# Two projections in a 256-token trunk change how high and low parts meet on TensorE

## The chip, the cores and the metric

The kernel runs on one core of a Trainium2 chip. The metric is the device time of one execution in microseconds. The core has TensorE (PE, with its weight loads listed apart as PEld), VectorE (DVE), ScalarE (ACT), GpSimd (POOL) and SyncE (SP), which here issues all bulk transfers from device memory (HBM). TensorE reads operands from on-chip memory (SBUF) and writes into PSUM, which has 8 banks of 128 partitions x 512 float32 columns; VectorE and ScalarE read results out of PSUM.

## The reference

Two layers over 256 tokens of width 1024, all in float32. Each layer: a token mixer, cross-attention into 256 memory tokens, and a feed-forward block (dense in layer 0, a routed mixture of 8 experts in layer 1).

```python
for l in range(DEPTH):
    h = rmsnorm(x, g_mix[l])
    z = h @ w_in[l]                                   # 1024 -> 4096
    gates = sigmoid(z[..., o_g:])
    y_pool = pool_mixer(u_pool, w_pool_group[l], pool_scale[l]) @ w_pool_out[l]    # 512 -> 1024
    y_conv = (b_gate * short_conv(c_gate * u_conv, conv_w[l])) @ w_conv_out[l]     # 512 -> 1024
    merged = gates[..., :D_MODEL] * y_pool + gates[..., D_MODEL:] * y_conv
    x = x + merged @ w_mix_out[l]
    h = rmsnorm(x, g_xattn[l]);  mem_n = rmsnorm(mem, g_mem[l])
    x = x + cross_attention(h, mem_n, w_xq[l], w_xk[l], w_xv[l], w_xo[l])   # k = mem_n @ w_xk[l]
    h = rmsnorm(x, g_ffn[l])
    x = x + (swiglu(h, ...) if l % 2 == 0 else moe_ffn(h, ...))
return rmsnorm(x, g_final)
```

## The kernel before

**Split operands.** Every float32 operand of a large product is split into a high part (rounded to the fast matmul type) and a low part (the rest). A product is the sum of three passes: high x high, high x low, low x high. Weights arrive in *units* of 1 MB (128 x 2048 elements) in six raw buffers, loaded by SP in a fixed order. For each unit ScalarE copies the high part (`split_to`, tile whi) and VectorE subtracts it to get the low part (wlo); there are three whi/wlo pairs, so the high part of unit n waits until unit n-3 has been used by TensorE. TensorE waits for `lo_ready` of a unit before it starts it and raises `unit_used` at its end. The order on each engine is the order in which the code is written; the three engines walk through the same units with counters `p.u` (units), `p.c` (PSUM pairs) and `p.q` (transpose banks).

**PSUM.** Banks 0 to 5 form three pairs that are used in turn (`take_pair` waits for `pair_free`); banks 6 and 7 take transposes in turn (`take_bank` waits for `tp_free`).

**Two ways to multiply with transposed output.** `chunk_t` (lines 1364 to 1385) issues, for each of 16 (k, d) blocks of a unit, three matmuls with 256 columns each; high and low parts lie in separate tiles (mem_hi, mem_lo; b_hi, b_lo), and the whole result gathers in one place, so that one engine reads it once. It is used for K (`w_xk`, 4 units a layer) and for the two branch output projections (`w_pool_out`, `w_conv_out`, 4 units a layer, called B units below: B0 to B3). `chunk_wide` (lines 1387 to 1407) is used for `w_in`, `w_xq` and the dense gate and up: the activation's high and low parts lie side by side in a_parts, one matmul with 512 columns multiplies both by the weight's high part, and one with 256 columns multiplies the high part by the weight's low part. Its result lies in two halves, which ScalarE copies (`wide_side`) and VectorE adds (`wide_sum`).

**Around the B units.** Before them TensorE computes the last gates; after them come the `w_mix_out` units M0 to M3 (`chunk_n`). M0 needs `merged_ready` 1, M1 needs `merged_ready` 2. VectorE multiplies each B unit's result by its gates (L1088), for the last two adds the two branches (L1094), ScalarE copies the sum's high part into a_parts, and VectorE subtracts for the low part (L933), which raises `merged_ready`.

**The start.** The memory tokens are normalised, transposed four 128 x 512 groups at a time in banks 6 and 7 (two, then two more once VectorE has emptied the first), scaled and split into mem_hi and mem_lo (`evac_norm`), and the first K unit starts. `keep_clock` issues small matmuls whose results nobody reads.

**The experts.** After layer 1's attention SP streams 192 expert units of 1792 KB through a ring of 12 places; a place is refilled when TensorE has used it.

## Time and profile before

| | us |
|---|---|
| median of 3 runs (lowest, highest) | 1538.47 (1538.39, 1539.16) |
| time of the profiled execution | 1538.15 |
| its span (first to last instruction) | 1536.1 |
| PE, busy in the span | 1506.7 |
| PEld | 972.8 |
| DVE | 549.2 |
| ACT | 407.7 |

The span is 2.05 us shorter than the time of the same execution. The ends of matmuls are modelled and they overlap, so a busy TensorE may be waiting for a fraction of a microsecond; the distance between the starts of matmuls tells its pace better than its busy time.

### The profile page before, as it was taken

The numbers are of one execution on the slowest core, as the hardware profiler recorded it, in microseconds if no ns is written. First come the engines' busy times: TensorE is split into PE (matmuls) and PEld (weight loads), VectorE is DVE, ScalarE is ACT, GpSimd is POOL, SyncE is SP. The second block draws the span as 40 slices with busy tenths as digits, with TensorE's granted clock in tenths as the row PEclk, the third lists the DMA queues.
The fourth block names the chain that finished last, engine by engine and source line by source line (L and its number), as shares of the span: only waits on it lengthen the run. The fifth ranks groups of instructions, "written<-read, shape, count | busy, mean of one in ns | idle before, by whom it ended". The sixth has DMA issues, their size and how long they took to land. (4 is left out here: it accounts for less than half of the span.)

```text
span 1536.1 us, 31153 instructions
## 1 busy us (share of the span) xinstructions
PE 1506.7 (98%) x14375; PEld 972.8 (63%) x14375; DVE 549.2 (36%) x641; ACT 407.7 (27%) x512; POOL 32.2 (2%) x118
## 2 busy tenths in 40 slices
PE   8999999999999999999999999999999999999996
PEld 8889888988888889886354343443543434435433
DVE  5576666565566767552021110110211101101112
ACT  6445455544445454541000000000000000000001
POOL 1000000000000000103000000000000000000000
PEclk9999999999999999999999999999999999999998
DMA  9655653547566555667989999999999999999993
GB/s 339 206 176 187 230 167 110 164 166 228 163 210 195 164 193 190 241 275 309 403 354 405 425 425 427 423 426 425 425 425 425 425 425 425 425 425 425 425 425 163
DMA packets 124967, 478.68 MB, mean 312 GB/s; under 512 B 6212, under 2 KB 72868, under 8 KB 100260
## 3 DMA queue, kind: packets, MB, share of 16 engines
q1 hardware_dynamic: 124836, 476.68, 79.5%
q8 instruction: 113, 1.85, 0.5%
q14 instruction: 18, 0.15, 0.0%
HBM read 475.61 MB, written 1.05 MB: 310 GB/s over the span
## 5 line engine op out<-in xcount | busy, mean ns | idle before, releaser
L1721 PE MATMUL ps<-unit,h_slots 128*32 128x448 f32 x5376 | 511.2, 540 | 0.0
L1721 PEld LDWEIGHTS ps<-unit,h_slots 128*32 128x32 f32 x5376 | 173.0, 110 | 321.6 <-issue 318.4
L1403 PE MATMUL ps<-a_parts,whi 128*128 128x512 f32 x992 | 344.1, 396 | 0.0
L928 DVE TENSOR_TENSOR wlo<-raw,whi 128x2048 fp32r<-128x2048 f32 (+1 forms) x116 | 259.1, 2236 | 122.0 <-ACT whi L591 121.6
L1743 PE MATMUL ps<-unit,act_tok 128*32 128x256 f32 x4704 | 259.3, 380 | 11.4 <-DVE act_tok L1299 8.9
L1403 PE MATMUL ps<-a_parts,wlo 128*128 128x256 f32 x992 | 267.0, 280 | 0.0
L591 ACT ACTIVATE whi<-raw 128x2048 fp32r<-128x2048 f32 (+1 forms) x116 | 216.5, 1867 | 67.1 <-PE ps L1421 53.1
L1743 PEld LDWEIGHTS ps<-unit,act_tok 128*32 128x32 f32 x4704 | 151.3, 110 | 119.9 <-DVE act_tok L1299 12.3
L1403 PEld LDWEIGHTS ps<-a_parts,whi 128*128 128x128 f32 x992 | 182.9, 188 | 38.2
L1403 PEld LDWEIGHTS ps<-a_parts,wlo 128*128 128x128 f32 x992 | 187.1, 189 | 5.4
L1295 DVE TENSOR_TENSOR act_tok<-act_tok,ps 128x896 f32<-128x896 f32 x18 | 19.2, 1067 | 352.3 <-PE ps L1721 352.3
L591 ACT ACTIVATE y_slots<-ps 32x256 f32<-32x256 f32 x38 | 14.2, 373 | 329.1 <-PE ps L1743 328.7
L1256 DVE COPY y_slots<-ps 32x256 f32<-32x256 f32 x38 | 16.1, 423 | 193.7 <-PE ps L1743 193.2
L1421 PE MATMUL ps<-whi,a_parts 128*128 128x512 f32 x256 | 79.8, 393 | 1.1 <-DVE a_parts L933 1.1
L884 ACT ACTIVATE act_tok<-ps 128x896 f32<-128x896 f32 x18 | 16.5, 917 | 237.9 <-PE ps L1721 237.9
L1421 PEld LDWEIGHTS ps<-whi,a_parts 128*128 128x128 f32 x256 | 47.6, 188 | 11.3 <-issue 1.9
L1421 PE MATMUL ps<-wlo,a_parts 128*128 128x512 f32 x128 | 49.9, 390 | 0.0
L591 ACT ACTIVATE h_slots<-ps 128x384 f32<-128x384 f32 (+1 forms) x8 | 3.3, 465 | 143.8 <-PE ps L1697 142.4
L1269 DVE TENSOR_TENSOR x_res<-x_res,ps 128x512 f32<-128x512 f32 x28 | 18.0, 684 | 55.5 <-PE ps L1773 55.5
L1381 PE MATMUL ps<-mem_hi,whi 128*128 128x256 f32 x128 | 36.5, 285 | 0.0
L1381 PE MATMUL ps<-mem_hi,wlo 128*128 128x256 f32 x128 | 36.3, 283 | 0.0
L1381 PE MATMUL ps<-b_hi,wlo 128*128 128x256 f32 x128 | 36.3, 283 | 0.0
(256 smaller groups left out, 1241.6 us busy)
## 6 DMA issues: line engine op xcount, KB each, us to landing
unit<-in_w_e_gate SPq DMA_DIRECT2D x64, 1792.0 KB, 28.5
unit<-in_w_e_up SPq DMA_DIRECT2D x64, 1792.0 KB, 27.2
unit<-in_w_e_down SPq DMA_DIRECT2D x64, 1792.0 KB, 28.9
raw<-in_w_in SPq DMA_DIRECT2D x32, 1024.0 KB, 5.4
raw<-in_w_ff_gate SPq DMA_DIRECT2D x10, 1024.0 KB, 5.4
raw<-in_w_ff_up SPq DMA_DIRECT2D x10, 1024.0 KB, 5.3
raw<-in_w_xk SPq DMA_DIRECT2D x8, 1024.0 KB, 5.1
raw<-in_w_xv SPq DMA_DIRECT2D x8, 1024.0 KB, 5.1
```

The costliest lines, as they stand in the source:

```text
L591: return act.activation(dst, src, ACT.Copy, scale=scale)
L884: act.activation(dst, src, ACT.Silu).then_inc(s["silu_ready"], 1)
L928: dve.tensor_tensor(wlo[n % SPL][:, 0:size], raw[n % RAW][:, 0:size], whi[n % SPL][:, 0:size].bitcast(F32), ALU.subtract).then_inc(s["lo_r ...
L1256: ins = dve.tensor_copy(y_rows(g, q), y_piece(g, q))
L1269: dve.tensor_tensor(xs, xs, bank(SCATTER_BANKS[n]), ALU.add).then_inc(s["xadd_done"], 1)
L1295: dve.tensor_tensor(dst, dst, src, ALU.mult).then_inc(s["act_ready"], 1)
L1381: ins = pe.matmul(o[:, d, :], w[wi][:, k, d * P:(d + 1) * P], xs[xi][:, k0 + k, :], start=first and d % 2 == 0, stop=last, skip_group_chec ...
L1403: ins = pe.matmul(o if whole else o[:, 0:SEQ], w, x_, start=k == 0 and whole, stop=k == nk - 1 and whole, skip_group_check=True)
L1421: ins = pe.matmul(o[:, t, 0:nn], xs[xi][:, k0 + k, t * P:(t + 1) * P], w[wi][:, k, :], start=j == 0 and k == 0 and n == 0, stop=j == n_uni ...
L1721: ins = pe.matmul(ps[q * QP:(q + 1) * QP, 2 * h + f, 0:HC], he[:, k, c0 + h * QP:c0 + (h + 1) * QP], w[:, q * QC + f * HC:q * QC + (f + 1) ...
L1743: ins = pe.matmul(o[q * QP:(q + 1) * QP, h * 256:(h + 1) * 256], act_t[:, h, j * QP:(j + 1) * QP], unit_t[i - part + u][:, c0:c0 + 256], s ...
```

## The change

K and the B units move from `chunk_t` to the wide form. mem_hi and mem_lo become the two halves of mem_parts, b_hi and b_lo those of b_parts. K weights are loaded as tall units (all 8 k blocks x 256 columns, rows of 1 KB, in place of 4 k blocks x 512 columns, rows of 2 KB). `keys` reads K's results with a ScalarE copy and a VectorE sum for each unit. The B units use a new `chunk_wide_rows`: a unit fills two PSUM pairs, one after the other, and ScalarE and VectorE bring both into a scratch tile mix_tmp (which lies over b_gateT and win_sum1) before the gates are multiplied. At the start all four transpose groups go to four banks (6, 7, 4, 5) without a wait, `keep_clock` has 5 calls in place of 10 there (a call shows as two matmuls in the trace), and the first weight unit is split in two halves of 1024 columns.

`chunk_t` is gone.

```diff
-    add_square(a["w_xk"][0])
+    def add_keys(l):
+        for c in range(D // C):
+            add_tall(a["w_xk"][l], c * C, C)
+
+    add_keys(0)
...
         if l == 0:
-            add_square(a["w_xk"][1])
+            add_keys(1)
...
-    Ml = place("mem_lo", [P, KD, SEQ], F32R)
+    M = place("mem_parts", [P, KD, 2, SEQ], F32R)
+    Mh, Ml = M[:, :, 0, :], M[:, :, 1, :]
     kT = place("kT", [P, KD, SEQ], F32)
     moe_top = at["top"]
     gT = place("gatesT", [P, 2 * KD, SEQ], F32)
-    Bh = place("b_hi", [P, KD, SEQ], F32R)
-    Bl = place("b_lo", [P, KD, SEQ], F32R)
+    B = place("b_parts", [P, KD, 2, SEQ], F32R)
...
+    mix_tmp = [place(f"mix_tmp{i}", [P, NG, SEQ], F32, place_of[n]) for i, n in enumerate(("b_gateT", "win_sum1"))]
...
+        FIRST_BANKS = (6, 7, 4, 5)
+        HALF_UNIT = UNIT // 2
...
-                def evac_norm(dst, row, lo=0, hi=KD // 2):
+                def evac_norm(dst, row, lo=0, hi=KD // 2, banks=(6, 7, 6, 7)):
 
                     for kk in range(lo, hi):
                         act.wait_ge(s["tp_done"], p.q + 1)
-                        src = bank(6 + p.q % 2).rearrange("p (k t) -> p k t", k=2)
...
+                def pair_side(dst, scale=1.0):
+
                     src = pair(p.c).rearrange("p (d h t) -> p d h t", d=2, h=2)[:, :, 1, :]
                     copy(dst, src, scale).then_inc(s["wide_side"], 1)
                     p.c += 1
...
-                split_to(0)
-                evac_norm(Mh, G_MEM)
+                act.wait_ge(raw_loaded[0], 16)
+                copy(whi[0][:, 0:HALF_UNIT], raw[0][:, 0:HALF_UNIT]).then_inc(s["hi_half"], 1)
+                copy(whi[0][:, HALF_UNIT:], raw[0][:, HALF_UNIT:]).then_inc(s["hi_ready"], 1)
+                p.u = 1
+                evac_norm(Mh, G_MEM, banks=FIRST_BANKS)
                 split_to(1)
...
-                ue = 1
-                for c in range(2):
-                    if c:
-                        norm_in(Ah, G_MIX, ue)
-                    chunk_in(ue)
-                    copy(kT[:, 4 * c:4 * c + 4, :], tiles_of(p.c)).then_inc(pair_free[p.c % 3], 1)
-                    p.c += 1
-                    ue += 2
+                def keys(row, ue):
+
+                    for h in range(NH):
+                        ue += 1
+                        if h == NH - 1:
+                            norm_in(Ah, row, ue)
+                        wide_side(kT[:, 2 * h:2 * h + 2, :], ue)
+                    return ue
+
+                ue = keys(G_MIX, -1)
...
-                    ue += 2
-                    p.c += 2
-                    for c in range(2):
-                        split_to(ue + 3 + c)
-                        act.wait_ge(s["merged_f"], 2 * l + c + 1)
-                        copy(Ah[:, 4 * c:4 * c + 4, :], gT[:, 4 * c:4 * c + 4, :]).then_inc(s["hi_evac"], 1)
-                        p.c += 1
-                    ue += 2
+                    for c in range(4):
+                        ue += 1
+                        split_to(ue + 2)
+                        if c >= 2:
+                            act.wait_ge(s["mix_prod"], 4 * l + c - 1)
+                        act.wait_ge(s["unit_used"], ue + 1)
+                        for d in (0, 2):
+                            pair_side(mix_tmp[c % 2][:, d:d + 2, :])
+                        if c >= 2:
+                            act.wait_ge(s["merged_f"], 2 * l + c - 1)
+                            copy(Ah[:, 4 * c - 8:4 * c - 4, :], gT[:, 4 * c - 8:4 * c - 4, :]).then_inc(s["hi_evac"], 1)
 
...
-                        for c in range(2):
-                            ue += 2
-                            if c:
-                                norm_in(Ah, G_FFN, ue)
-                            chunk_in(ue)
-                            copy(kT[:, 4 * c:4 * c + 4, :], tiles_of(p.c)).then_inc(pair_free[p.c % 3], 1)
-                            p.c += 1
-
+                        ue = keys(G_FFN, ue)
...
+
+                def pair_sum(dst, scale=1.0):
+
+                    pair_sum.n += 1
+                    dve.wait_ge(s["wide_side"], pair_sum.n)
                     src = pair(p.c).rearrange("p (d h t) -> p d h t", d=2, h=2)[:, :, 0, :]
...
                 normalize(xm, xm)
+                dve.wait_ge(s["hi_half"], 1)
+                dve.tensor_tensor(wlo[0][:, 0:HALF_UNIT], raw[0][:, 0:HALF_UNIT], whi[0][:, 0:HALF_UNIT].bitcast(F32), ALU.subtract)
+                dve.wait_ge(s["hi_ready"], 1)
+                dve.tensor_tensor(wlo[0][:, HALF_UNIT:], raw[0][:, HALF_UNIT:], whi[0][:, HALF_UNIT:].bitcast(F32), ALU.subtract
+                                  ).then_inc(s["lo_ready"], 1)
+                p.u = 1
                 dve.wait_ge(s["consts_used"], 1)
-                split_to(0)
-                evac_norm(Ml, Mh, G_MEM)
+                evac_norm(Ml, Mh, G_MEM, banks=FIRST_BANKS)
                 split_to(1)
...
-                norm_in(Al, Ah, G_MIX, ue)
+
+                def keys(row, ue):
+
+                    for h in range(NH):
+                        ue += 1
+                        if h == NH - 1:
+                            norm_in(Al, Ah, row, ue)
+                        wide_sum(kT[:, 2 * h:2 * h + 2, :], ue)
+                    return ue
+
+                ue = keys(G_MIX, -1)
                 ue += 2
...
 
                         split_to(ue + (2 if c < 3 else 1))
-                        dve.wait_ge(s["unit_used"], ue + 1)
+                        for d in (0, 2):
+                            pair_sum(mix_tmp[c % 2][:, d:d + 2, :])
                         if c == 0:
 
                             dve.wait_ge(s["gates_done"], 4 * (l + 1))
+                        dve.wait_ge(free(p.c - 1), u_free(p.c - 1))
                         g = gT[:, 4 * c:4 * c + 4, :]
-                        ins = dve.tensor_tensor(g, g, tiles_of(p.c), ALU.mult)
-                        ins.then_inc(free(p.c), 1)
-                        p.c += 1
+                        dve.tensor_tensor(g, g, mix_tmp[c % 2][:], ALU.mult).then_inc(s["mix_prod"], 1)
                         if c >= 2:
-                            dve.wait_ge(free(p.c - 1), u_free(p.c - 1))
+                            dve.wait_ge(s["mix_prod"], 4 * l + c + 1)
                             m = gT[:, 4 * (c - 2):4 * (c - 2) + 4, :]
                             dve.tensor_tensor(m, m, g, ALU.add).then_inc(s["merged_f"], 1)
...
                         normalize(x, xn)
-                        ue += 2
-                        split_to(ue + 2)
-                        p.c += 1
-                        ue += 2
-                        norm_in(Al, Ah, G_FFN, ue)
...
                                     w = (hi if whole else lo)[:, k, d * P:(d + 1) * P]
-                                    x_ = A[:, k, :, :].rearrange("p h t -> p (h t)") if whole else A[:, k, 0, :]
...
                         p.c += 1
+                        if between and j == 0:
+                            between()
+
+                def chunk_wide_rows(xs):
+
+                    _, _, nk, _, nn = units[p.u]
+                    hi, lo = parts(p.u)
+                    pe.wait_ge(s["lo_ready"], p.u + 1)
+                    for d0 in (0, 2):
+                        take_pair()
+                        for k in range(nk):
+                            for d in (d0, d0 + 1):
+                                o = pair(p.c)[:, (d - d0) * C:(d - d0 + 1) * C]
+                                for whole in ((True, False) if k == 0 else (False, True)):
+                                    w = (hi if whole else lo)[:, k, d * P:(d + 1) * P]
+                                    x_ = xs[:, k, :, :].rearrange("p h t -> p (h t)") if whole else xs[:, k, 0, :]
+                                    ins = pe.matmul(o if whole else o[:, 0:SEQ], w, x_, start=k == 0 and whole,
+                                                    stop=k == nk - 1 and whole, skip_group_check=True)
+                        p.c += 1
+                    ins.then_inc(s["unit_used"], 1)
+                    p.u += 1
 
...
-                def transposes(src, lo, hi):
+                def transposes(src, lo, hi, banks=(6, 7, 6, 7)):
 
                     for kk in range(lo, hi):
-                        take_bank()
-                        b = bank(6 + p.q % 2).rearrange("p (k t) -> p k t", k=2)
+                        if banks[kk] >= 6:
+                            take_bank()
...
                 q_mem = p.q
-                transposes(xm, 0, 2)
-                keep_clock(10)
-                transposes(xm, 2, KD // 2)
+                transposes(xm, 0, KD // 2, FIRST_BANKS)
+                keep_clock(5)
                 ready = normed(q_mem)
-                chunk_t(2, MEM, ready)
+                chunk_wide(ready, M)
                 q_h = p.q
-                chunk_t(2, MEM, already, lambda: transposes(xn, 0, 2))
+                chunk_wide(already, M, lambda: transposes(xn, 0, 2))
...
                     for c in range(2):
-                        chunk_t(1, XB, already)
+                        chunk_wide_rows(B[:, 0:NG, :, :])
                     pe.wait_ge(s["yc_ready"], l + 1)
                     for c in range(2):
-                        chunk_t(1, (Bh[:, 4:8, :], Bl[:, 4:8, :]), already)
+                        chunk_wide_rows(B[:, NG:, :, :])
                     ready = once(s["merged_ready"], lambda k: 2 * l + k // 4 + 1)
                     for c in range(2):
...
-                        chunk_t(2, MEM, ready)
+                        chunk_wide(ready, M)
                         q_h = p.q
-                        chunk_t(2, MEM, already, lambda: transposes(xn, 0, 2))
+                        chunk_wide(already, M, lambda: transposes(xn, 0, 2))
```

ScalarE from its last gate results of layer 0 to the copies of the merged sum; the numbers behind whi and raw are buffers, whi is the high part of a unit, a_parts the merged sum's high part. Before:

```order
L698 ACTIVATE gatesT<-gatesT 128x1024
L591 ACTIVATE whi_65<-raw_61 128x2048
L591 ACTIVATE whi_67<-raw_62 128x2048
L591 ACTIVATE whi_63<-raw_56 128x2048
L591 ACTIVATE a_parts<-gatesT 128x4x256
L591 ACTIVATE whi_65<-raw_57 128x2048
L591 ACTIVATE a_parts<-gatesT 128x4x256
```

After:

```order
L717 ACTIVATE gatesT<-gatesT 128x1024
L600 ACTIVATE whi_63<-raw_59 128x2048
L600 ACTIVATE mix_tmp_93<-ps 128x512 x2
L600 ACTIVATE whi_65<-raw_60 128x2048
L600 ACTIVATE mix_tmp_94<-ps 128x512 x2
L600 ACTIVATE whi_61<-raw_54 128x2048
L600 ACTIVATE mix_tmp_93<-ps 128x512 x2
L600 ACTIVATE a_parts<-gatesT 128x4x256
L600 ACTIVATE whi_63<-raw_55 128x2048
L600 ACTIVATE mix_tmp_94<-ps 128x512 x2
L600 ACTIVATE a_parts<-gatesT 128x4x256
```

Two copies out of PSUM stand behind each unit's high part, and the last two stand between unit M1's high part (whi_63<-raw_55) and the second copy of the merged sum.

VectorE in the same place, from the second B unit's product with its gates to the second low part of the merged sum. Before:

```order
L1088 TENSOR_TENSOR gatesT<-gatesT,ps 128x1024
L928 TENSOR_TENSOR wlo_64<-raw_56,whi_63 128x2048
L1088 TENSOR_TENSOR gatesT<-gatesT,ps 128x1024
L1094 TENSOR_TENSOR gatesT<-gatesT 128x1024
L933 TENSOR_TENSOR a_parts<-gatesT,a_parts 128x4x256
L1088 TENSOR_TENSOR gatesT<-gatesT,ps 128x1024
L1094 TENSOR_TENSOR gatesT<-gatesT 128x1024
L928 TENSOR_TENSOR wlo_66<-raw_57,whi_65 128x2048
L933 TENSOR_TENSOR a_parts<-gatesT,a_parts 128x4x256
```

After:

```order
L1121 TENSOR_TENSOR gatesT<-gatesT,mix_tmp_94 128x1024
L943 TENSOR_TENSOR wlo_62<-raw_54,whi_61 128x2048
L1014 TENSOR_TENSOR mix_tmp_93<-mix_tmp_93,ps 128x512 x2
L1121 TENSOR_TENSOR gatesT<-gatesT,mix_tmp_93 128x1024
L1125 TENSOR_TENSOR gatesT<-gatesT 128x1024
L948 TENSOR_TENSOR a_parts<-gatesT,a_parts 128x4x256
L1014 TENSOR_TENSOR mix_tmp_94<-mix_tmp_94,ps 128x512 x2
L1121 TENSOR_TENSOR gatesT<-gatesT,mix_tmp_94 128x1024
L1125 TENSOR_TENSOR gatesT<-gatesT 128x1024
L943 TENSOR_TENSOR wlo_64<-raw_55,whi_63 128x2048
L948 TENSOR_TENSOR a_parts<-gatesT,a_parts 128x4x256
```

Two sums of 512 columns stand ahead of each product with the gates; the order of the rest is as it was.

## Rows read from the trace of the kernel before

**Rows 1.** Waits of TensorE, whole span: total, times, longest us

```profile
PE ps L1462 <- DVE mem_lo L953: 1.3, 1, 1.3
PE ps L1421 <- DVE a_parts L933: 1.1, 2, 0.5
```

**Rows 2.** TensorE's timeline, first matmul of each stage: start, us, operation

```profile
10.02 1.20 PE L1462 MATMUL ps<-ident,mem_norm 128*128 128x128 f32 x8
11.06 2.40 PE L1483 MATMUL ps<-ident 128*128 128x128 f32 x20
14.73 1.44 PE L1462 MATMUL ps<-ident,mem_norm 128*128 128x128 f32 x8 [1.27 <-DVE mem_lo L953]
15.92 0.36 PE L1381 MATMUL ps<-mem_hi,whi 128*128 128x256 f32 x1
33.28 1.03 PE L1462 MATMUL ps<-ident,x_norm 128*128 128x128 f32 x8
51.70 0.39 PE L1403 MATMUL ps<-a_parts,whi 128*128 128x512 f32 x1
118.86 1.46 PE L1512 MATMUL ps<-pooledT,w_group 128*128 128x256 f32 x6
142.99 0.28 PE L1381 MATMUL ps<-b_hi,whi 128*128 128x256 f32 x1
166.01 0.63 PE L1421 MATMUL ps<-whi,a_parts 128*128 128x512 f32 x2
172.18 0.70 PE L1421 MATMUL ps<-whi,a_parts 128*128 128x512 f32 x2 [0.54 <-DVE a_parts L933]
```

**Rows 3.** Forms of ScalarE and VectorE, 0 to 560 us: busy, mean ns

```profile
L996 DVE TENSOR_TENSOR gatesT<-gatesT,ps 128x512 f32<-128x512 f32 x12 | 8.2, 683 | 4.8 <-ACT gatesT L591 4.8
L591 ACT ACTIVATE gatesT<-ps 128x512 f32<-128x512 f32 x13 | 7.8, 597 | 28.4 <-PE ps L1403 28.4
L928 DVE TENSOR_TENSOR wlo<-raw,whi 128x1024 fp32r<-128x1024 f32 x4 | 4.9, 1220 | 0.0
L591 ACT ACTIVATE whi<-raw 128x1024 fp32r<-128x1024 f32 x4 | 4.2, 1054 | 0.0
```

**Rows 4.** VectorE's timeline, third B unit and after, layer 0

```profile
160.45 1.22 DVE L1088 TENSOR_TENSOR gatesT<-gatesT,ps 128x1024 f32<-128x1024 f32 x1 [1.46 <-PE ps L1381]
161.71 1.23 DVE L1094 TENSOR_TENSOR gatesT<-gatesT 128x1024 f32<-128x1024 f32 x1
164.06 1.23 DVE L933 TENSOR_TENSOR a_parts<-gatesT,a_parts 128x1024 fp32r<-128x1024 f32 x1 [1.13 <-ACT a_parts L591]
168.61 2.28 DVE L928 TENSOR_TENSOR wlo<-raw,whi 128x2048 fp32r<-128x2048 f32 x1
170.81 1.22 DVE L933 TENSOR_TENSOR a_parts<-gatesT,a_parts 128x1024 fp32r<-128x1024 f32 x1
```

**Rows 5.** ScalarE's timeline in the same stretch

```profile
162.97 1.06 ACT L591 ACTIVATE a_parts<-gatesT 128x1024 fp32r<-128x1024 f32 x1 [6.30 <-DVE gatesT L1094]
163.94 1.90 ACT L591 ACTIVATE whi<-raw 128x2048 fp32r<-128x2048 f32 x1
```

**Rows 6.** ScalarE's and VectorE's timelines at the start

```profile
9.58 1.91 ACT L591 ACTIVATE whi<-raw 128x2048 fp32r<-128x2048 f32 x1 [0.89 <-DMA raw<-in_w_xk]
13.81 1.65 DVE L953 SCALAR_TENSOR_TENSOR mem_lo<-ps,consts_t,mem_hi 128x256 fp32r<-128x256 f32 x4
```

**Rows 7.** Stretches: us, busy by engine, TensorE clock, DMA share, GB/s

```profile
10.00:20.00 10.00, 8.60 (x72) 7.99 (x71) 6.93 (x11) 7.53 (x15) 0.00 (x0) 1.00 1.05 390
20.00:30.00 10.00, 10.00 (x86) 10.00 (x85) 6.99 (x5) 7.17 (x9) 1.09 (x3) 1.00 1.09 357
```

**Rows 8.** The page, GB/s in 40 slices of 38.4 us

```profile
GB/s 339 206 176 187 230 167 110 164 166 228 163 210 195 164 193 190 241 275 309 403 354 405 425 425 427 423 426 425 425 425 425 425 425 425 425 425 425 425 425 163
```

**Rows 9.** The tail: a stretch as in rows 7, then TensorE's timeline

```profile
1524.00:1525.00 1.00, 1.00 (x3) 0.76 (x4) 0.47 (x1) 0.00 (x0) 0.00 (x0) 0.50 0.00 0
...
1523.86 0.79 PE L1884 MATMUL ps<-y_hi,sel_slot 64*128 64x512 f32 x1 [3.45 <-DVE y_lo L1845]
```

More of the change, by code:

```diff
@@ L216, in moe @@
         return t
-    work = [place_of["mem_hi"], place_of["mem_hi"] + 16384]
+    work = [place_of["mem_parts"], place_of["mem_parts"] + 16384]
     fixed = [m0 + 6144, m0 + 8192]
@@ L1365, in parts, with chunk_wide @@
                     return unit_view(whi[u % SPL], u), unit_view(wlo[u % SPL], u)
-                def chunk_t(n_units, xs, ready, between=None):
-                    take_pair()
-                    o = tiles_of(p.c)
-                    for j in range(n_units):
-                        _, k0, nk, _, nn = units[p.u]
-                        w = parts(p.u)
-                        pe.wait_ge(s["lo_ready"], p.u + 1)
-                        for k in range(nk):
-                            ready(k0 + k)
-                            for d in range(nn // P):
-                                for n, (wi, xi) in enumerate(PASSES):
-                                    first = j == 0 and k == 0 and n == 0
-                                    last = j == n_units - 1 and k == nk - 1 and n == 2
-                                    ins = pe.matmul(o[:, d, :], w[wi][:, k, d * P:(d + 1) * P], xs[xi][:, k0 + k, :],
-                                                    start=first and d % 2 == 0, stop=last, skip_group_check=True)
-                        ins.then_inc(s["unit_used"], 1)
-                        p.u += 1
-                        if between and j == 0:
-                            between()
-                    p.c += 1
-                def chunk_wide(ready):
-                    for _ in range(2):
+                def chunk_wide(ready, xs=A, between=None):
+                    for j in range(2):
                         take_pair()
```

30 lines of the change are left out of this document (18 added, 12 removed).

## The prediction

> **What bounds the kernel now.** I read the waits of TensorE first. Once it has started, and up to the experts, TensorE waits for another engine in two places only: 1.3 us at the start, for a transpose bank that VectorE has to empty, and 0.5 us in each layer before the second half of `w_mix_out`, for VectorE's low part of the merged sum [rows 1]. Elsewhere one stage follows the other without a gap in TensorE's timeline [rows 2]. So the trunk costs what TensorE's matmuls cost, and a stage gets shorter in two ways alone: a faster pace of the matmuls, or less of those waits. What the reader should see next is how thin the cover is behind the B units: VectorE's chain from B2's result to the last low part runs from 160.45 to 172.03, and ScalarE's copies fill its gaps [rows 4, 5], and TensorE wants that low part at 171.64. Whatever is added to that chain is paid at full price.
>
> Behind the trunk the experts' weights stream at 425 GB/s for half of the span [rows 8]. The first of them is asked for behind the last trunk unit, and the ring's places come free by TensorE's own progress; so a trunk that ends later by some time moves stream, experts and end by the same time. I count every microsecond of the trunk in full.
>
> **Pace.** Three passes: the four B units take 142.99 to 166.01, 5.755 us each, and three K units 15.92 to 33.28, 5.79 each [rows 2]. Wide form: twelve `w_in` units take 51.70 to 118.86, 5.597 us each [rows 2]. Both push 768 columns per block through TensorE; the wide form loads two weight tiles where the other loads three. The gain is 0.16 to 0.19 us a unit. K has 8 units in both layers: 8 x 0.175 = 1.4 us gained. The B units' 8 x 0.16 is inside the chain below. The Trainium skill, page "TensorE: Matmul & The Clock Gate", section "Wait — 56ns, not 53.3ns?", puts a matmul's pace at columns / 2.4 plus about 2.5 ns; by that a block would gain one such 2.5 ns, 256 blocks 0.6 us and not 2.7. The rows show 4 times as much, and I go by the rows.
>
> ScalarE's and VectorE's extra work for K (a copy of 0.60 us and a sum of 0.68 us a unit [rows 3], in place of one copy for two units) is hidden: in a unit of 5.6 us they also split one unit, 1.90 and 2.28 us [rows 4, 5]. Without that cover it would cost 0.6 us a unit.
>
> **The start.** Now the first K matmul is at 15.92 [rows 2]. After the change, transposes and `keep_clock` no longer set it: sixteen transposes from 10.02 at 1.04 per eight, then five calls, 1.2 us, end at about 13.3 [rows 2]. The weight unit does. ScalarE began its high part at 9.58, having waited 0.89 us for the transfer [rows 6]. Rows of 1 KB move more slowly: the stretch with mostly 2 KB rows shows 390 GB/s, the next, where tall units come in, 357 [rows 7], which is 0.25 us more for 1 MB; so 9.83. Two copies of 1.05, overlapping by 0.09 (rows 5 shows this overlap between ScalarE's instructions), end at 10.88 and 11.84. VectorE's two halves of 1.22 [rows 3] end at 12.13 and 13.27 (overlap 0.08). Then it makes the low parts of the first transpose group, two of the four instructions that take 1.65 [rows 6]: 13.19 to 14.04. TensorE starts 0.12 later, at 14.16: 1.76 us gained. If the unit comes no later than now it is 2.0; if it comes 0.6 later, 1.4. Ahead of the second K unit the distance stays as it is, since all that leads to its low part moves forward too.
>
> **The B units.** I count from B0's first matmul, which is 0. Before: B2's result is with VectorE at 17.46, M0 starts at 23.02, M1 at 29.19 [rows 2, 4]. After:
>
> 1. B2 ends: 3 x 5.597 = 16.79, plus the 0.20 from pace to result that the same sum gives for before (17.46 - 3 x 5.755): 16.99.
> 2. ScalarE copies two pairs, 0.60 each, the second starting 0.50 after the first: done at 17.62 and 18.12. The first pair has been full for half a unit, but both copies wait for `unit_used`, which is raised at the unit's end.
> 3. VectorE sums them, 0.69 each: the second 18.25 to 18.93.
> 4. Product with the gates 1.22, adding the branches 1.23, ScalarE's high part 1.06, VectorE's low part 1.23 [rows 4, 5], with 0.03 to 0.04 at each hand-over: 20.19, 21.46, 22.55, 23.81. That is `merged_ready` 1. B3 ended at 22.39: **a new wait of 1.4 us.** M0 starts at 23.95.
> 5. Next on ScalarE is not B3's copy but M1's high part: 22.46 to 24.36. Behind it the two copies: 24.86, 25.36. VectorE's second sum: 25.49 to 26.18; product 27.44; addition 28.70.
> 6. VectorE then makes M1's low part, 2.28, as before ahead of the sum's low part: 30.90; the sum's low part 30.82 to 32.04. `merged_ready` 2 came at 29.04 before.
> 7. M1 starts 0.15 later (172.03 to 172.18 now [rows 2, 4]): 32.19 in place of 29.19. M0, which takes 5.63 (166.01 to 171.64), ends at 29.58: **the second wait is 2.5 us in place of 0.5.**
>
> So each layer loses 3.0 us here, the B units' better pace already taken off. The cause is two sums and two copies that stand one behind the other in a chain that had no slack, and a copy queued behind a 1.9 us split. Pairs of PSUM don't bind: each B unit's second pair needs the first pair of the unit before, summed 1.2 us or more ahead of its use. After M1 the low parts of M2 and M3 have a unit of 5.4 us to be ready in, and the delay does not grow. A second `take_pair` in each B unit is an already fulfilled wait; I leave it at nothing, up to 0.1 us a layer.
>
> **Sum.** -1.8 (start) - 1.4 (K) + 2 x 3.0 (B units) = +2.8 us. The profiled execution, 1538.15 with a span of 1536.1, becomes 1541.0 with a span of 1538.9. The median of the runs is 0.3 above the profiled execution: 1541.3. That is 0.18%, just within the 0.2% (3.1 us) which is about what a measurement of this kernel can tell from no change.
>
> **Rivals.**
>
> - *The chain as above*, with its terms somewhat off: the start 1.4 to 2.0, K 1.2 to 1.6, each layer 2.8 to 3.3. Own range +2.0 to +4.0, 1540.5 to 1542.5. Chance 0.62, of which 0.35 lies within 0.2%.
> - *More waits than I found* (slower). The early units arrive later because of 1 KB rows, or K's sums come in the way of the third and fourth unit's low parts: one stall of 1 to 2 us, 1543. For it: the transfer queue is full at 1.05 of its share from 10 to 30 us [rows 7]. Against it: TensorE uses 1 MB in 5.6 us, which is 190 GB/s, half of what arrives. Chance 0.15.
> - *The clock falls in the new waits* (slower). At the tail TensorE stood idle for 3.45 us, and the granted clock is 0.50, the 1.2 GHz level, in the stretch behind it [rows 9]. My longest wait is 2.5 us; nothing in the trace shows an idle stretch of that length. If half of M1's 5.6 us ran at half clock it would cost 2.8 us a layer: 1546.9. The same page of the Trainium skill, section "What's actually happening", says that the halved clock is the default and activity lifts it; the tail agrees. Chance 0.07.
> - *Columns alone set the pace* (slower). Both forms push the same columns, so no unit would gain: K 1.4, and three B units ahead of the chain 0.5 a layer, 2.4 us more, 1543.7. The units' own rows speak against it. Chance 0.03. The rule of the Trainium skill quoted above would come near this.
> - *The later trunk is absorbed* in the experts' stream, if its end were set by something that does not move. Then at least layer 1's 3.0 us vanish: 1538.3. I see no such fixed point; the stream has to wait for `merged_ready` as well. Chance 0.07.
> - *The chain does not bind* (faster). If the stretch from B2's end to M1, 15.2 us in my count and 11.7 now, grew so little that M1 were not late, the waits of rows 1 would be gone: -1.8 - 1.4 - 1.3 - 1.1 = -5.6, 1532.9. It decides for faster only below about 12.2 us, which takes VectorE's product from SBUF in half its time; the addition of two SBUF operands takes 1.23 [rows 4], no less than the product from PSUM. Chance 0.06.
>
> **How the numbers follow.** Faster by over 0.2%: 0.06. Within: 0.35 of the first and 0.07 of the absorbed case, and 0.02 of the second's cheap end: 0.44. Slower: the rest, 0.50. The predicted time is the first case's, 1541.3. The range leaves out the clock and the faster case and the far end of the absorbed one: 1539.9 to 1543.9.
>
> **What the changed profile would show.** Right: waits of TensorE for a_parts (L948) of about 1.4 and 2.5 us in each layer, 7.8 in all in place of 1.1; no wait for mem_lo; first K matmul near 14.2; K and B units at 5.6 us; ScalarE's copies of B3 directly behind a 1.9 us split. Wrong: M1 less than 31 us behind B0, a granted clock below 1.00 after M0, a TensorE wait between 14 and 40 us, or a first K matmul later than 14.8.

## The result, and the profile after

| | before | after |
|---|---|---|
| median of the runs, us | 1538.43 (1537.38 to 1540.5, 15 runs) | 1542.66 (1541.1 to 1545.06, 15 runs) |
| ratio, 95% interval | | 1.0031 (1.0024 to 1.0038) |
| profiled execution, us | 1538.15, span 1536.1 | 1543.7, span 1541.6 |
| mean granted clock of the runs | 0.995 to 0.997 (the 64 runs beside the experiments) | 0.993 to 0.996 |

The change costs 4.2 us, 0.31%. The runs of after differ more than those of before, and the longer ones have the lower granted clock: the five at 0.993 have a mean of 1544.57, the four at 0.996 one of 1541.88. The profiled execution is one of the five.

The waits of TensorE after (total, times, longest us), against [rows 1]:

```profile
PE ps L1449 <- DVE a_parts L948: 7.9, 4, 2.5
...
PE ps L1410 <- DVE mem_parts L968: 0.9, 1, 0.9
```

The wait for the low part of the merged sum, L948, went from 2 times and 1.1 us in all to 4 times and 7.9 us. The 1.3 us for mem_lo are gone; the first K matmul waits 0.9 us for the low part of the memory instead. TensorE's timeline, first matmul of each stage as in [rows 2], layer 0 and then layer 1 from 576 us:

```profile
12.02 1.28 PE L1514 MATMUL ps<-ident 128*128 128x128 f32 x10
14.18 0.47 PE L1410 MATMUL ps<-mem_parts,whi 128*128 128x512 f32 x1 [0.87 <-DVE mem_parts L968]
...
140.53 0.39 PE L1431 MATMUL ps<-b_parts,whi 128*128 128x512 f32 x1
164.57 0.70 PE L1449 MATMUL ps<-whi,a_parts 128*128 128x512 f32 x2 [1.43 <-DVE a_parts L948]
172.77 1.19 PE L1449 MATMUL ps<-whi,a_parts 128*128 128x512 f32 x2 [2.51 <-DVE a_parts L948]
...
```

M0 comes 24.04 us behind B0 and M1 32.24, where they came 23.02 and 29.19 behind it. Up to the first `w_in` unit the change is 2.46 us ahead of before (49.24 against 51.70). In VectorE's timeline in the same stretch, against [rows 4], two sums (L1014) stand ahead of each product:

```profile
158.27 1.29 DVE L1014 TENSOR_TENSOR mix_tmp<-mix_tmp,ps 128x512 f32<-128x512 f32 x2 [0.93 <-ACT mix_tmp L600]
159.59 1.23 DVE L1121 TENSOR_TENSOR gatesT<-gatesT,mix_tmp 128x1024 f32<-128x1024 f32 x1
160.85 1.23 DVE L1125 TENSOR_TENSOR gatesT<-gatesT 128x1024 f32<-128x1024 f32 x1
163.20 1.23 DVE L948 TENSOR_TENSOR a_parts<-gatesT,a_parts 128x1024 fp32r<-128x1024 f32 x1 [1.13 <-ACT a_parts L600]
165.49 1.28 DVE L1014 TENSOR_TENSOR mix_tmp<-mix_tmp,ps 128x512 f32<-128x512 f32 x2 [1.06 <-ACT mix_tmp L600]
166.80 1.22 DVE L1121 TENSOR_TENSOR gatesT<-gatesT,mix_tmp 128x1024 f32<-128x1024 f32 x1
...
171.41 1.22 DVE L948 TENSOR_TENSOR a_parts<-gatesT,a_parts 128x1024 fp32r<-128x1024 f32 x1
```

At the start ScalarE's and VectorE's timelines, against [rows 6], show the two halves of the first unit:

```profile
9.79 2.01 ACT L600 ACTIVATE whi<-raw 128x1024 fp32r<-128x1024 f32 x2 [1.04 <-DMA raw<-in_w_xk]
...
10.88 1.23 DVE L1032 TENSOR_TENSOR wlo<-raw,whi 128x1024 fp32r<-128x1024 f32 x1 [0.70 <-ACT whi L600]
12.03 1.22 DVE L1034 TENSOR_TENSOR wlo<-raw,whi 128x1024 fp32r<-128x1024 f32 x1
13.16 3.22 DVE L968 SCALAR_TENSOR_TENSOR mem_parts<-ps,consts_t,mem_parts 128x256 fp32r<-128x256 f32 x8
```

And in the stretch of the B units ScalarE's timeline, against [rows 5]: B3's two copies wait for the end of the 1.89 us split.

```profile
162.11 1.06 ACT L600 ACTIVATE a_parts<-gatesT 128x1024 fp32r<-128x1024 f32 x1 [3.39 <-DVE gatesT L1125]
163.08 1.89 ACT L600 ACTIVATE whi<-raw 128x2048 fp32r<-128x2048 f32 x1
164.88 1.07 ACT L600 ACTIVATE mix_tmp<-ps 128x512 f32<-128x512 f32 x2
```

What the waits don't show is the clock behind them. Stretches of after, columns as in [rows 7] (the last three are TensorE's granted clock, as a share of 2.4 GHz, the DMA share and GB/s):

```profile
170.00:172.00 2.00, 0.26 (x2) 0.00 (x0) 2.00 (x2) 2.00 (x2) 0.00 (x0) 1.00 0.00 0
172.00:174.00 2.00, 1.23 (x3) 1.06 (x4) 2.00 (x2) 1.98 (x2) 0.00 (x0) 0.64 0.67 210
174.00:176.00 2.00, 2.00 (x6) 1.52 (x6) 2.00 (x2) 0.00 (x0) 0.00 (x0) 0.50 0.91 317
176.00:178.00 2.00, 2.00 (x10) 1.64 (x9) 1.03 (x1) 0.00 (x0) 0.00 (x0) 1.00 0.95 330
...
608.00:612.00 4.00, 3.19 (x9) 2.54 (x10) 4.00 (x3) 2.02 (x2) 0.00 (x0) 0.68 0.81 264
612.00:616.00 4.00, 4.00 (x17) 3.24 (x17) 1.07 (x1) 0.00 (x0) 0.00 (x0) 0.89 1.01 334
```

M1 begins at 172.77 and runs at 0.50, the 1.2 GHz level, until about 176; 6 matmuls begin in 174 to 176, 10 in the next two us. In layer 1 it is the same. So from M1 to the first transposes of xn, the normalised tokens, it takes 23.38 us in layer 0 and 23.48 in layer 1, where before takes 21.85 in both (172.18 to 194.03, 604.20 to 626.05).

Where after stands against before in the profiled executions adds up like this: first K matmul 1.74 earlier; first `w_in` unit 2.46 earlier; M1 of layer 0 0.59 later, which is 3.05 for the chain; transposes of xn 2.12 later, 1.53 for the clock; B0 of layer 1 1.57 later, 0.55 regained in K; M1 4.61 later, 3.04 for the chain; transposes of xn 6.24 later, 1.63 for the clock. At the transposes of x_res, 691.40 against 685.16, it is still 6.24, and at the start of the last matmul that reads an expert's down unit 6.2 (1526.2 against 1520.0). From there to the end after takes 15.4 us and before 16.1, so 5.5 are left at the end of the span. The profiled executions of the other kernels take 15.3 to 16.0 for this last part, so the 0.7 is no more than they differ by.

### The profile page after: what moved, and what is told of

It is laid out like the page before. It is cut to its first block and busy times, and to the rows that moved or that the text cites. A ratio compares the mean times of both kernels' runs of the same rounds, so it can differ in the third digit from the quotient of the medians.

```text
span 1541.6 us, 30672 instructions
## 1 busy us (share of the span) xinstructions
PE 1507.4 (98%) x14109; PEld 958.6 (62%) x14109; DVE 564.1 (37%) x666; ACT 415.8 (27%) x533; POOL 32.2 (2%) x118
## 5 line engine op out<-in xcount | busy, mean ns | idle before, releaser
L943 DVE TENSOR_TENSOR wlo<-raw,whi 128x2048 fp32r<-128x2048 f32 (+2 forms) x115 | 256.9, 2235 | 112.0 <-ACT whi L600 111.7
L600 ACT ACTIVATE whi<-raw 128x2048 fp32r<-128x2048 f32 (+2 forms) x117 | 216.5, 1853 | 59.5 <-PE ps L1449 57.2
L1410 PEld LDWEIGHTS ps<-a_parts,whi 128*128 128x128 f32 x992 | 182.8, 188 | 38.4
L1285 DVE COPY y_slots<-ps 32x256 f32<-32x256 f32 x38 | 16.1, 424 | 195.2 <-PE ps L1773 194.8
L1410 PE MATMUL ps<-mem_parts,whi 128*128 128x512 f32 x128 | 45.0, 397 | 0.9 <-DVE mem_parts L968 0.9
L1431 PE MATMUL ps<-b_parts,whi 128*128 128x512 f32 x128 | 44.0, 396 | 0.0
L1449 PE MATMUL ps<-whi,mem_parts 128*128 128x512 f32 x128 | 39.8, 392 | 0.0
```

Of the source, the lines that this page charges most:

```text
L600: return act.activation(dst, src, ACT.Copy, scale=scale)
L943: dve.tensor_tensor(wlo[n % SPL][:, 0:size], raw[n % RAW][:, 0:size], whi[n % SPL][:, 0:size].bitcast(F32), ALU.subtract).then_inc(s["lo_r ...
L1285: ins = dve.tensor_copy(y_rows(g, q), y_piece(g, q))
L1410: ins = pe.matmul(o if whole else o[:, 0:SEQ], w, x_, start=k == 0 and whole, stop=k == nk - 1 and whole, skip_group_check=True)
L1431: ins = pe.matmul(o if whole else o[:, 0:SEQ], w, x_, start=k == 0 and whole, stop=k == nk - 1 and whole, skip_group_check=True)
L1449: ins = pe.matmul(o[:, t, 0:nn], xs[xi][:, k0 + k, t * P:(t + 1) * P], w[wi][:, k, :], start=j == 0 and k == 0 and n == 0, stop=j == n_uni ...
```

## The experiments

Three sets, each on one chip together with before (1538.32, 1538.48 and 1538.26 us). For each the same distances are read from TensorE's timeline of layer 0, as in [rows 2]:

| kernel | median, us | ratio, 95% interval | M0 behind B0 | M1 behind B0 | M1 to xn |
|---|---|---|---|---|---|
| before | 1538.4 | | 23.02 | 29.19 | 21.85 |
| after | 1542.66 | 1.0031 (1.0024 to 1.0038) | 24.04 | 32.24 | 23.38 |
| e1_b_three_pass | 1535.97 | 0.9984 (0.9975 to 0.9993) | 23.02 | 29.32 | 21.85 |
| e2_b_wide_alone | 1547.86 | 1.0058 (1.0044 to 1.0071) | 24.04 | 32.24 | 23.47 |
| e3_busy_waits | 1543.35 | 1.0032 (1.0019 to 1.0044) | 23.95 | 33.26 | 21.89 |
| e5_copies_first | 1538.82 | 1.0004 (0.9995 to 1.0013) | 24.03 | 31.08 | 21.85 |
| e4_start_alone | 1536.51 | 0.9987 (0.9978 to 0.9996) | 23.02 | 29.32 | 21.85 |
| e6_half_signal | 1536.51 | 0.9988 (0.9979 to 0.9997) | 23.38 | 29.97 | 21.89 |
| e7_fill_second | 1541.46 | 1.0020 (1.0011 to 1.0030) | 24.04 | 32.15 | 21.90 |
| e8_fill_first | 1543.63 | 1.0037 (1.0024 to 1.0049) | 23.94 | 32.23 | 23.48 |
| e9_two_wide | 1535.00 | 0.9979 (0.9970 to 0.9988) | 22.74 | 29.07 | 21.89 |

My theory was that of the prediction (start and K gain, the B units' chain loses), with one addition from the profile after: the fall of the clock is a cost of its own. The intervals of the ratios below are 2 to 4 us wide, while distances in the timeline repeat to 0.1 us from kernel to kernel, so the readings rest on these. The rivals were that it is the start or K that loses, and that the clock comes down for a reason other than the waits.

**e1_b_three_pass**: all of the change but the wide B units.

```diff
-                                o = pair(p.c)[:, (d - d0) * C:(d - d0 + 1) * C]
-                                for whole in ((True, False) if k == 0 else (False, True)):
...
+                                for n, (wi, xi) in enumerate(PASSES):
+                                    ins = pe.matmul(tiles_of(p.c)[:, d - d0, :], (hi, lo)[wi][:, k, d * P:(d + 1) * P],
+                                                    xs[:, k, xi, :], start=k == n == 0 and d == d0,
+                                                    stop=k == nk - 1 and n == 2, skip_group_check=True)
```

> The changed kernel with the B units back to three passes of 256 columns (each unit's result in two PSUM pairs, multiplied by the gates straight from PSUM); start and K stay changed. Theory (the B units' longer chain on ScalarE and VectorE, and the clock that falls in its wait, cost all that is lost): TensorE's waits for a_parts fall back to about 0.5 us a layer, the clock stays 1.00 behind them, and the kernel is 3.0 us faster than before the change (1.8 at the start, 1.4 in K, 0.1 given back). Rival (1 KB rows or K's extra sums cost something that I don't see): it is less than 1.5 us faster than before, or slower.

Measured 1535.97, 2.35 below before, where 3.0 were expected; in the profiled execution the first K matmul comes at 14.88, 1.04 earlier than before and not 1.8. Its timeline at M0 and M1:

```profile
164.26 0.63 PE L1445 MATMUL ps<-whi,a_parts 128*128 128x512 f32 x2
170.56 0.70 PE L1445 MATMUL ps<-whi,a_parts 128*128 128x512 f32 x2 [0.67 <-DVE a_parts L944]
```

No wait ahead of M0, 0.67 ahead of M1, and the clock is 1.00 behind it. So the whole loss of the change comes with the wide B units: 1542.66 less 1535.97, 6.7 us. The wait of 0.67 is 0.13 longer than the 0.54 of before. The gates are multiplied in two halves here, which was expected to give 0.1 back.

**e2_b_wide_alone**: the start and K as before, the B units wide (K with the three-pass code on tall units, `FIRST_BANKS = (6, 7, 6, 7)`, the first unit whole, `keep_clock(10)`).

```diff
-        FIRST_BANKS = (6, 7, 4, 5)
+        FIRST_BANKS = (6, 7, 6, 7)
-                chunk_wide(ready, M)
+                chunk_three(ready, MEM)
```

> Only the B units are changed: start as before (two transpose groups, ten calls, two more groups; whole first unit), K in three passes (on tall units). Theory: the two B stages alone cost 6.1 us, and between nothing and 3 us more where the granted clock falls behind the 2.5 us wait: 1544.5 to 1547.5 where before is 1538.4. Rival (the loss is spread over the change): less than 4 us.

Measured 1547.86, 9.5 above before and 0.4 above the range expected. The waits are those of the change (1.43 and 2.51 in layer 0, 1.43 and 2.48 in layer 1), and in the stretch behind M1 the clock is down again:

```profile
176.00:178.00 2.00, 2.00 (x7) 1.63 (x6) 2.00 (x2) 0.67 (x1) 0.00 (x0) 0.63 1.03 357
178.00:180.00 2.00, 2.00 (x6) 1.51 (x6) 1.71 (x1) 0.00 (x0) 0.00 (x0) 0.52 0.82 272
```

At the transposes of x_res its profiled execution is 9.54 us behind before, and that is 0.2 at the start, 6.1 for two chains and 3.2 for the clock. This execution, 1550.06, is the slowest of the five. It then loses another 2.5 us among the experts: the matmuls that read their down units take 739.5 us from the first to the last, where before takes 737.0. The trace has two things there. TensorE's idle time ahead of them that is put down to a transfer is 7.9 us in place of 6.3, and behind the last such wait, 2.25 us, the clock falls once more (0.54 from 1528 to 1530). I have no experiment that parts the two. So e1's gain and e2's loss don't add up to the change by their medians (-2.35 and +9.5 against +4.2). By the timeline they do up to the transposes of x_res: 9.54 less 1.95 at the start (first K matmul at 16.13 and 14.18), 1.3 in K and 0.1 of the clock is after's 6.24. The five runs of e2 have granted clocks of 0.992 to 0.994, as low as the longest runs of after.

**e3_busy_waits**: after, with 6 identity matmuls ahead of the wait for `merged_ready` 1 and 10 ahead of that for 2, so that TensorE is not idle.

```diff
+                        if first_product[0] and k in (0, 4):
+                            for _ in range(6 if k == 0 else 10):
+                                pe.matmul(bank(6)[:, 0:P], ident[:], ident[:], start=True, stop=True)
```

> The changed kernel, with matmuls on the identity that nobody reads ahead of TensorE's two waits for merged_ready in each layer (6 and 10 calls, about 1.4 and 2.3 us), so that TensorE is busy while it waits. Theory: the waits' ends stay where they are (M1 starts 32.2 us behind B0), but the clock stays at 1.00 behind them, M1 takes 5.5 us in place of 7 where the clock had fallen, and the kernel is 1.5 to 3 us faster than the changed one, still 2 to 3 slower than before, with a narrower spread. Rival (the clock has no share, M1 is slow for another reason): no difference to the changed kernel.

Measured 1543.35, no better than after. In its timeline (each identity matmul shows as two):

```profile
171.83 2.50 PE L1561 MATMUL ps<-ident 128*128 128x128 f32 x20 [1.31 <-DVE wlo L943]
174.08 0.71 PE L1449 MATMUL ps<-whi,a_parts 128*128 128x512 f32 x2
```

The granted clock is 1.00 in all stretches behind it, and M1 to xn takes 21.89. But TensorE stands in an earlier wait first, for M1's own low weights (L943); the filler starts only behind that and runs past the moment when a_parts is there, so M1 comes 33.26 behind B0, 1.0 later than in after. What the clock gave back the filler used up, so neither the 1.5 to 3 us nor the end of the wait came out as expected. What did is the narrower spread: the six runs lie within 0.7 us (1542.89 to 1543.61), those of after within 4. e7 below mends the filler's place.

**e5_copies_first**: after, with ScalarE's copies of B3 ahead of M1's high part.

```diff
-                        split_to(ue + 2)
+                        if c < 3:
+                            split_to(ue + 2)
...
                         for d in (0, 2):
                             pair_side(mix_tmp[c % 2][:, d:d + 2, :])
+                        if c == 3:
+                            split_to(ue + 2)
```

> The changed kernel with one thing moved: ScalarE makes its two copies of B3's result ahead of M1's high part, not behind it. Theory (the copies queued behind a 1.9 us split are part of the chain): M1 starts 1.3 us earlier in each layer (30.9 behind B0), the second wait is 1.2 us, too short for the clock to fall, and the kernel is 2.6 us faster than the changed one by the chain and up to 3 more by the clock: 0 to 1 us slower than before. Rival (VectorE's sums alone make the chain): less than 1 us gained.

Measured 1538.82, 3.8 below after, and the same as before. M1 comes at 31.08, 1.16 earlier:

```profile
164.78 0.70 PE L1452 MATMUL ps<-whi,a_parts 128*128 128x512 f32 x2 [1.42 <-DVE a_parts L951]
171.83 0.70 PE L1452 MATMUL ps<-whi,a_parts 128*128 128x512 f32 x2 [1.36 <-DVE a_parts L951]
```

The copy behind the split was 1.16 of the chain's 3.05 us. Twice 1.16 is 2.3. The other 1.5 of the 3.8 I put down to the clock, which is 1.00 in both layers behind two waits of 1.4; no run shows that share alone.

**e4_start_alone**: K and B in three passes, the new start kept (`chunk_three` as in e2, `FIRST_BANKS` and the halved first unit as in after).

> Only the start of the change: the first weight unit converted in two halves and the memory transposes in four more banks; K and the branch units keep three matmuls of 256 columns. Theory (start gains, K's pace gains apart from it, both small): first K matmul at 14.2 to 14.9 us in place of 16.0, all later stages shifted by that alone, no wait of more than 1.3 us at a branch unit, M1 29.2 us behind B0 and granted clock 1.00 there; 1536.5 to 1537.3, that is 1.2 to 2.0 below before, and e1_b_three_pass, which has K's wide columns too, lies about 1.4 below this one (less if the pace of K is not what gained there). Rival (the start is absorbed by a later transfer or wait): 1538.3, and the whole gain of e1_b_three_pass is K's.

```profile
14.13 0.47 PE L1430 MATMUL ps<-mem_parts,whi 128*128 128x256 f32 x2 [0.56 <-DVE mem_parts L966]
```

Measured 1536.51, 1.97 below before (0.6 to 3.4 by the interval), with the first K matmul 1.79 earlier: that agrees with a start that is worth what it gains there. Against e1, K's wide form shows from the first K matmul to B0 as 126.36 in place of 127.08 us, and from B0 of layer 0 to B0 of layer 1 as 431.66 in place of 432.28: 0.72 and 0.62, 1.34 us in all. The medians differ by 0.54 only, and their intervals overlap. In the profiled executions e1's first K matmul comes 0.75 later (14.88 against 14.13); whether that holds for the other runs no trace shows.

**e6_half_signal**: after with one more semaphore, `b_half`, at the half of each B unit. Its first copy and, for B3, the first sum are made while TensorE does the unit's second half; M1's high part comes behind B3's copies.

```diff
+                        if d0 == 0:
+                            ins.then_inc(s["b_half"], 1)
...
+                        act.wait_ge(s["b_half"], 4 * l + c + 1)
+                        pair_side(mix_tmp[c % 2][:, 0:2, :])
...
+                            if c == 2:
+                                pair_sum(mix_tmp[1][:, 0:2, :])
```

> The change with one more semaphore at the half of each branch unit: the copy and the first sum of its first pair of blocks are made while TensorE works on the second pair, and M1's high part comes behind the copies of B3. Theory (the wait is the chain of copies and sums behind a unit's last matmul, and half of that chain can lie under the unit itself): M0 about 23.4 and M1 about 29.9 us behind B0 (23.95 and 32.19 in the change), waits of about 1.0 and 0.9 us, granted clock 1.00 behind M1, M1 to the transposes of xn 21.9; 1536.5 to 1537.2, that is 1.2 to 2 below before. Rival (VectorE has no room: the sums only move and push the low parts of the next unit): M1 at 31 or later behind B0, 1538.5 to 1539.

Measured 1536.51, as the theory has it: 6.2 below after with all B units still wide. e5's move is part of this kernel, so the signal's own share is what it gains on e5: M0 at 23.38 and not 24.03, M1 at 29.97 and not 31.08. VectorE's timeline now has one sum behind B2's end, and B3's first one ahead of the low part:

```profile
158.57 0.69 DVE L1020 TENSOR_TENSOR mix_tmp<-mix_tmp,ps 128x512 f32<-128x512 f32 x1 [0.86 <-ACT mix_tmp L600]
159.30 1.23 DVE L1127 TENSOR_TENSOR gatesT<-gatesT,mix_tmp 128x1024 f32<-128x1024 f32 x1
160.56 1.23 DVE L1131 TENSOR_TENSOR gatesT<-gatesT 128x1024 f32<-128x1024 f32 x1
161.70 0.68 DVE L1020 TENSOR_TENSOR mix_tmp<-mix_tmp,ps 128x512 f32<-128x512 f32 x1
162.91 1.23 DVE L954 TENSOR_TENSOR a_parts<-gatesT,a_parts 128x1024 fp32r<-128x1024 f32 x1 [0.53 <-ACT a_parts L600]
```

The wait ahead of M0 is 0.77 and that ahead of M1 0.86. VectorE had the room; the chain's place was what cost.

**e7_fill_second**: e3 mended: no filler ahead of M0; ahead of M1 5 identity matmuls before the wait for its low weights and 4 behind it.

> The change with 5 identity matmuls ahead of the low-part wait of M1 and 4 behind it, none ahead of M0: TensorE is kept busy in the longer wait of the two, and they are short enough to end before a_parts is there. Theory (after's wait chain stands, and the fall of the granted clock behind it is a cost of its own): M1 still 32.2 us behind B0, granted clock 1.00 behind it, M1 to the transposes of xn 21.9 in place of 23.4; 1539.5 to 1541.0, that is 1.5 to 3 below the change and 1.2 to 2.7 above before. Rival (the clock fell for another reason than the idle stretch, so filler does nothing): 1542.5, M1 to xn 23.4.

```profile
170.06 1.27 PE L1560 MATMUL ps<-ident 128*128 128x128 f32 x10
171.50 1.16 PE L1560 MATMUL ps<-ident 128*128 128x128 f32 x8 [0.17 <-DVE wlo L943]
172.63 0.73 PE L1449 MATMUL ps<-whi,a_parts 128*128 128x512 f32 x2
```

The stretch behind it, columns as in [rows 7]:

```profile
174.00:176.00 2.00, 2.00 (x11) 1.65 (x10) 2.00 (x2) 0.00 (x0) 0.00 (x0) 1.00 0.93 307
```

M1 starts where it did (32.15), the clock stays at 1.00 in both layers, and M1 to xn takes 21.90. Measured 1541.46: 1.2 below after, where 1.5 to 3 were expected, and the intervals of the two ratios overlap. That the clock costs 1.5 us where it falls is shown by the distance from M1 to xn (23.38 us behind an M1 at 32.24, 21.90 behind one at 32.15), and not by the medians. This is the kernel that my sum describes, the chain without the fall of the clock at the B units, and the sum said 1541.3.

**e8_fill_first**: after with 6 identity matmuls ahead of M0 alone, so that only the longer wait is idle.

> The change with 6 identity matmuls in the wait ahead of M0 alone; the 2.5 us ahead of M1 stay idle. If that one wait alone brings the clock down: M1 at 32.2 behind B0, granted clock 0.5 for some 2 us behind M1, M1 to xn 23.4, 1542.5 as the change. If both waits within 10 us are needed for it: granted clock 1.00 behind M1, M1 to xn 21.9, 1539.5 to 1541. In either case the waits' own 2 x 3.0 us per pass of the branches stay.

```profile
172.00:174.00 2.00, 1.09 (x4) 0.96 (x5) 2.00 (x2) 2.00 (x2) 0.00 (x0) 0.93 0.59 194
174.00:176.00 2.00, 2.00 (x6) 1.54 (x5) 2.00 (x2) 0.12 (x1) 0.00 (x0) 0.50 0.95 330
...
608.00:612.00 4.00, 2.94 (x13) 2.46 (x14) 4.00 (x3) 2.28 (x2) 0.00 (x0) 1.00 0.76 259
```

Measured 1543.63, like after. In layer 0 the clock fell behind a wait of 2.58 us, in layer 1 it did not behind one of 2.55, and M1 to xn takes 23.48 and 21.89 us there: the cost of the fall within one execution. So the long wait alone is enough to bring it down, but does not do so each time, and neither of the two expectations holds as it stands.

**e9_two_wide**: B0 and B1 wide, B2 and B3, for whose results the merged sum waits, in three passes.

```diff
+                        if c < 2:
+                            act.wait_ge(s["unit_used"], ue + 1)
+                            for d in (0, 2):
+                                pair_side(mix_tmp[c][:, d:d + 2, :])
+                        else:
+                            p.c += 2
...
-                        chunk_wide_rows(B[:, NG:, :, :])
+                        chunk_wide_rows(B[:, NG:, :, :], False)
```

> The change with B0 and B1 wide and B2 and B3, whose results the merged memory of M0 and M1 waits for, in three matmuls of 256 columns. Theory (the wide form gains TensorE some 0.18 us a unit, which is kept where no wait stands behind the unit; the copies and sums of B2 and B3 were the whole loss): M0 at 22.7 and M1 at 29.0 us behind B0 (23.02 and 29.32 with all four in three passes), wait ahead of M1 0.7 or less, granted clock 1.00 there, M1 to the transposes of xn 21.9; 0.3 a layer better than all in three passes, so 1535.5 to 1536.7, 1.8 to 3 below before. Rival (the sums of B0 and B1 push the low parts of later weights, so that TensorE waits for those or for a_parts): M1 at 29.4 to 30.5 behind B0 and 1536.5 to 1538.

```profile
164.10 0.63 PE L1466 MATMUL ps<-whi,a_parts 128*128 128x512 f32 x2
170.43 0.70 PE L1466 MATMUL ps<-whi,a_parts 128*128 128x512 f32 x2 [0.70 <-DVE a_parts L949]
```

M0 at 22.74 and M1 at 29.07, 0.28 and 0.25 better than with four three-pass units. 1535.00 is the lowest median of all, 3.3 below before, 0.5 below the range expected and 7.7 below after; between it and e1 or e6, which were in other sets, the intervals of the ratios overlap.

## Why the prediction was right, and where not

**The chain of the B units: right.** Predicted 23.95 and 32.19 behind B0 with waits of 1.4 and 2.5; measured 24.04 and 32.24 with 1.43 and 2.51 in layer 0, and M1 is 3.05 us a layer later against B0 where 3.0 were counted. (By the prediction's own figures, M1 at 32.19 and the end of M0 at 29.58, the second wait would be 2.6.) e1 shows that this comes with the wide form of these units alone. Both causes named are shown: the copy behind the 1.9 us split (e5, 1.16 us), and the copies and sums that all come behind the unit's end (e6, which moves half of them ahead, brings M1 from e5's 31.08 to 29.97).

**The start: right.** 14.16 predicted, 14.18 measured, and e4 measures it alone at 1.97 us. Each step of the count held: the high part began at 9.79 (9.83 counted), the two low halves and then the memory's low parts followed on VectorE without a gap, those at 13.16 (13.19). In the nine kernels with this start the first K matmul comes at 14.06 to 14.94, and in all nine it comes 4.38 or 4.39 us behind ScalarE's first high part, which begins at 9.67 to 10.56, when the first unit has arrived. So the unit does set the start, as I counted, but its arrival varies by 0.9 us, and my range for it, 1.4 to 2.0 gained, was too narrow: e1 and e9 gain 1.0.

**K: right.** 1.4 predicted; e1 against e4 gives 1.34 in TensorE's timeline, and after against before 0.72 and 0.55. By the pace rule of the Trainium skill, page "TensorE: Matmul & The Clock Gate", section "Wait — 56ns, not 53.3ns?" (about 2.5 ns for each matmul beside its columns), I estimate a gain of 0.3 us for K's 128 blocks. The trace does not agree with that here: it has 1.3.

**The sum against the whole.** -1.8, -1.4 and +6.0 gave +2.8 and 1541.3. With the measured terms, 1.74, 1.3 and 6.1, it is +3.1, and e7, in which the clock stays up behind M1, measures 1541.46. The change itself measures 1542.66: inside the range, but 0.16 us outside the first case's own range. That the whole lies inside is in part luck: the sum has no term for the clock, 1.2 us by the medians of after and e7, and five of the fifteen runs, 1544.33 to 1545.06, lie above the range's end of 1543.9. The 0.2 us between e7 and the sum are closer than the start's 0.9 us and the intervals allow one to claim.

**The step that failed is the rival "the clock falls in the new waits"**, which had a chance of 0.07 and is true together with the first case. I had set it aside since "nothing in the trace shows an idle stretch of that length", and TensorE's waits in before do have nothing between 1.5 us (for a transfer, late among the experts) and 3.45; that was no evidence against it, only the lack of evidence, and the stretch of 3.45 with a clock of 0.50 behind it [rows 9] was the nearest row above. A granted clock below 1.00 after M0 stood among my own signs of being wrong, and the profile after has it in both layers. The chance should have been that of a bound between two rows, near one half. The price was off the other way: 2.8 us a layer was counted for 5.6 us of half clock, but the clock came back earlier, and it cost 1.5 to 1.6. Over all runs the effect looks smaller still: 1.2 us between the medians of after and e7. That fits e8, where one of two such waits left the clock up; how often it falls in runs without a trace is not shown.

**The other rivals fell.** The price of the faster one was off by itself: it took off 1.3 us for the start's wait, which the start's 1.8 already holds. There is no TensorE wait between 14 and 40 us, so no stall of the early units. Pace by columns alone is excluded by e1 against e4 and by e9. The later trunk was not absorbed: 6.24 us at the transposes of x_res are 5.5 at the end of the span.

## What to carry to other kernels

A form that is faster on TensorE and leaves its result in two pieces moves work to the engines behind it. Where a stage's result is wanted at once, take the form with the shortest way from the last matmul to the consumer, and the faster one where a unit of cover stands behind it (e9); or signal the first half early (e6). When the sum shows a new wait, price the clock behind it as a term of its own, and look in an engine's queue for what stands ahead of the instruction that the chain waits for (e5).

## What the runs showed of the hardware that was not expected

The granted clock fell to 0.50, the 1.2 GHz level, in the stretch behind TensorE waits of 2.51 us, which themselves came some 6 us behind a wait of 1.43: in both layers of after and of e2 (2.48 us in e2's layer 1). It stayed at 1.00 behind two waits of 1.42 and 1.36 (e5). With the first wait filled it fell behind one wait of 2.58 and not behind one of 2.55 in the same execution (e8). Each of these falls cost about 1.5 us. Waits for a transfer near the end of the experts show the same doubt. In e2 the clock falls behind one of 2.25 us, and in e4 it stays at 1.00 behind one of 2.42, each of them behind a wait of 0.61 and a burst of the same 48 matmuls. First e2, then e4:

```profile
1527.14 5.35 PE L1793 MATMUL ps<-unit,act_tok 128*32 128x256 f32 x64 [2.25 <-DMA unit<-in_w_e_down]
1528.00:1530.00 2.00, 2.00 (x25) 1.00 (x20) 0.00 (x0) 0.00 (x0) 0.00 (x0) 0.54 0.04 8
...
1516.48 3.66 PE L1791 MATMUL ps<-unit,act_tok 128*32 128x256 f32 x64 [2.42 <-DMA unit<-in_w_e_down]
1518.00:1519.00 1.00, 1.00 (x24) 0.64 (x20) 0.00 (x0) 0.00 (x0) 0.00 (x0) 1.00 0.00 0
```

So between 2.2 and 2.6 us the length of a wait alone does not decide it.

In the experts' part of after it fell once more, though the waits there are 0.3 and 0.6 us and the same as in before, whose profiled execution shows no fall there:

```profile
1418.00:1420.00 2.00, 2.00 (x21) 1.23 (x23) 0.56 (x1) 0.00 (x0) 0.00 (x0) 0.61 1.01 430
```

e7 shows the same at 1416. What decides it is open. That fall leaves no loss in the time: from the first to the last matmul that reads a down unit after takes 736.9 us and before 737.0. TensorE's idle time ahead of these matmuls that is put down to a transfer is 2.6 us in after and 6.3 in before, so the slower matmuls seem to have used up time in which TensorE would have waited for transfers; no experiment shows this by itself.
